# A 35,000-instruction transformer kernel: the second attention woven with the query projection, the rope angles moved forward, the last norm one tile ahead

## The reference

```python
cos, sin = rope_tables(positions)
...
proj = h @ w_q                                    # 1024 columns: 12 heads of 64, 256 memory query columns
q = apply_partial_rope(proj[..., :768], cos, sin) # rotates 16 of the 64 columns of a head
mix_out = sliding_window_attention(q, shared_k, shared_v, sinks)
mem_o = memory_attention(proj[..., 768:], mem_k, mem_v)
x = x + concatenate([mix_out, mem_o]) @ w_out
x = x + swiglu(rms_norm(x, ln_ffn), w_gate_up, w_down)
```

## Time and profile before

| | us |
|---|---|
| median of 3 runs | 2669.25 |
| lowest and highest | 2666.16, 2669.93 |
| the profiled execution, time | 2663.3 |
| the profiled execution, span | 2661.5 |
| TensorE busy | 2560.2 (96%) |
| VectorE busy | 1520.8 (57%) |
| ScalarE busy | 1043.8 (39%) |
| POOL busy | 978.9 (37%) |
| mean granted TensorE clock | 0.982 |

### The profile page before, as it was taken

The page is one execution under the profiler, slowest core; times in us unless marked ns, Lnnn a source line. Parts: engine busy times, 40 slices in busy tenths (PEclk is TensorE's granted clock), DMA queues, the critical chain, the costliest instruction groups (busy, mean ns, idle before and its releaser), DMA issues.

```text
span 2661.5 us, 35966 instructions
## 1 busy us (share of the span) xinstructions
PE 2560.2 (96%) x14072; PEld 2017.0 (76%) x14072; DVE 1520.8 (57%) x1968; ACT 1043.8 (39%) x1609; POOL 978.9 (37%) x259
## 2 busy tenths in 40 slices
PE   8999979999999899999989999999999998899998
PEld 7777938888877578888867777786658877688886
DVE  5736756542438746433266689973565784644244
ACT  5444544222232643222243355533454553432222
POOL 0346823444443024444433433341005552144443
PEclk9999979999999999999999999999999999899999
DMA  5225512222222012222233333334333332222222
GB/s 184 95 80 178 190 63 80 95 96 100 102 98 88 31 48 95 95 95 95 97 108 115 122 128 122 119 135 142 99 117 136 126 127 70 73 95 95 97 99 89
DMA packets 72391, 280.58 MB, mean 105 GB/s; under 512 B 9892, under 2 KB 27646, under 8 KB 45124
## 3 DMA queue, kind: packets, MB, share of 16 engines
q1 hardware_dynamic: 59875, 259.72, 28.7%
q10 hardware_dynamic: 12384, 19.03, 2.0%
HBM read 259.25 MB, written 19.40 MB: 105 GB/s over the span
## 4 chain that ended last, share of the span: by engine, by line
PE 71%; issue 17%; POOL 5%; DVE 4%; ACT 2%; DMA 0%; POOLq 0%; DVEq 0%; ACTq 0%; SPq 0%
PE banks L585 14%; PE banks L586 14%; PE banks L587 14%; POOL w_lo L3376 4%; PE banks L2752 2%; PE banks L1058 2%; PE banks L1057 2%; PE banks L1056 2%; PE banks L2760 2%; PE banks L1962 1%; PE banks L2863 1%; PE banks L2861 1%; PE banks L2862 1%; PE banks L2774 1%; PE banks L2507 1%
## 5 line engine op out<-in xcount | busy, mean ns | idle before, releaser
L3376 POOL TENSOR_TENSOR w_lo<-raw,w_hi 128x2048 fp32r<-128x2048 f32 x164 | 757.3, 4618 | 1337.9 <-ACT w_hi L564 1251.8
L585 PE MATMUL banks<-hn_hi,w_hi 128*128 128x512 f32 x1880 | 740.0, 394 | 21.0 <-DVE hn_lo L2275 7.8
L586 PE MATMUL banks<-hn_lo,w_hi 128*128 128x512 f32 x1880 | 735.5, 391 | 0.0
L587 PE MATMUL banks<-hn_hi,w_lo 128*128 128x512 f32 x1880 | 734.8, 391 | 0.0
L564 ACT ACTIVATE w_hi<-raw 128x2048 fp32r<-128x2048 f32 x180 | 345.0, 1917 | 607.4 <-PE banks L587 480.3
L585 PEld LDWEIGHTS banks<-hn_hi,w_hi 128*128 128x128 f32 x1880 | 355.1, 189 | 116.4 <-issue 32.5
L587 PEld LDWEIGHTS banks<-hn_hi,w_lo 128*128 128x128 f32 x1880 | 355.2, 189 | 74.7
L586 PEld LDWEIGHTS banks<-hn_lo,w_hi 128*128 128x128 f32 x1880 | 355.3, 189 | 72.6
L1001 DVE TENSOR_TENSOR hid_lo<-prod,hid_hi 128x512 f32 x62 | 281.4, 4538 | 117.8 <-ACT hid_hi L965 117.8
L998 DVE TENSOR_TENSOR prod<-sg,banks 128x512 f32<-128x512 f32 x62 | 42.6, 687 | 239.6 <-PE banks L587 239.6
L585 PE MATMUL banks<-hid_hi,w_hi 128*128 128x512 f32 x416 | 163.1, 392 | 3.3 <-POOL w_lo L3376 2.3
(11 more groups left out here) (582 smaller groups left out, 4064.8 us busy)
## 6 DMA issues: line engine op xcount, KB each, us to landing
raw<-in_W SPq DMA_DIRECT2D x202, 1024.0 KB, 4.8
oh_early<-codes SPq DMA_DIRECT2D x88, 128.0 KB, 3.0
extra<-in_W SPq DMA_DIRECT2D x8, 1024.0 KB, 4.7
spill<-cs ACTq DMA_DIRECT2D x32, 256.0 KB, 2.3
spill<-mem_q ACTq DMA_DIRECT2D x32, 256.0 KB, 2.7
oh_late<-codes SPq DMA_DIRECT2D x40, 128.0 KB, 2.8
grp<-spill SPq DMA_DIRECT2D x8, 512.0 KB, 4.5
grp<-spill SPq DMA_DIRECT2D x16, 256.0 KB, 4.8
```

The source lines that it names most:

```text
L585: pe.matmul(out, wh, xh(k), start=(k == 0), stop=False)
L586: pe.matmul(out, wh, xl(k), start=False, stop=False)
L587: mm = pe.matmul(out, wl, xh(k), start=False, stop=(k == nkt - 1))
L3376: pool.tensor_tensor(w_lo[:, u % 2, :], raw[:, u % 2, :], w_hi[:, u % 2, :].bitcast(F32), ALU.subtract).then_inc(S("w_lo"), 1)
```

## The change

1. **Weaving.** Query units 1 to 3 are done in half-jobs of 12 matmuls (half the k-steps of one output tile). After half-job q of unit i comes pair step 4i + q - 5, so that pairs 0 to 10 stand between the half-jobs, and pairs 11 to 18 (the last three without scores) follow as before. In a woven step TensorE makes values, transposes, scores, in this order. All woven scores use banks 2 and 3 (before, pairs took 4, 5 and 2, 3 in turn). The ropes stand where table `ROPES` says. ScalarE instead of VectorE evacuates the query tiles.
2. **Rope angles.** The 16 angle steps go behind the first six tiles of the down projection `dn02`: 3, 3, 3, 3, 2, 2. ScalarE issues the four loads ahead of that stage. The sines come directly behind the norm, before the next `prep_hi`.
3. **Last norm.** VectorE shifts tile j + 1 before it subtracts tile j.

```diff
+WOVEN = 11
+ROPES = {(0, 3): (6,), (1, 0): (0, 1), (1, 2): (2,), (2, 0): (3,), (2, 2): (4,), (3, 0): (5,)}
+ROPE_BANK = {6: 4, 0: 5, 1: 1, 2: 0, 3: 1, 4: 0, 5: 1}
+def pair_after(i, q):
+    p = 4 * i + q - 5
+    return p if 0 <= p < WOVEN else None
...
+    def pair_step(p):
+        if p < PAIRS:
+            for s in range(2):
+                k.add(("pair", p, s), (2 if p < WOVEN or p % 2 == 0 else 0) + s)
...
@@ dve_squares
+                if name == "dn02":
+                    rope_angles(v, min(16, 3 * k - max(0, k - 4)), min(16, 3 * k + 3 - max(0, k - 3)))
@@ act_ffn, down
+                    if f == 0:
+                        full(a, ("unit", U["dn01", 3], 1))
+                        for ap, load in ((rcol, "rcol"), (posi, "posi"), (perm, "perm"), (band, "band")):
+                            a.dma_start(ap[:, :], I[load]).then_inc(S("land_rope"), 16)
                     act_squares(a, name, ("norm", 3 + 3 * f), x_of, sq_tmp)
@@ dve_h2
+            shifted(0)
+            for j in range(KT):
+                if j + 1 < KT:
+                    shifted(j + 1)
+                taken(v, ("h2", j))
                 v.wait_ge(S("ada_hi"), KT + j + 1)
                 v.tensor_tensor(hn_lo[:, j, :], ring[:, j % 3, :], hn_hi[:, j, :].bitcast(F32), ALU.subtract)\
                     .then_inc(S("ada_lo"), 1)
...
+        def pe_pair_step(pe, p):
+            if WOVEN <= p < PAIRS:
+                pe_pair_scores(pe, p)
+            if p >= 3:
+                pe_pair_values(pe, p - 3)
+            if 2 <= p < PAIRS + 2:
+                pe_pair_turned(pe, p - 2)
+            if p < WOVEN:
+                pe_pair_scores(pe, p)
+        def pe_query_half(pe, i, q):
+            u, t = U["swaq", i], q // 2
+            key = ("unit", u, t)
+            if q == 0:
+                pe.wait_ge(S("w_lo"), u + 1)
+            hi, lo = W3(w_hi, u % 2), W3(w_lo, u % 2)
+            if q % 2 == 0:
+                open_bank(pe, key)
+            for k in range(4 * (q % 2), 4 * (q % 2) + 4):
...
+        def pe_queries(pe):
+            unit_jobs(pe, U["swaq", 0], 0, lambda k: t_hi[:, k, :], lambda k: t_lo[:, k, :], KT, ready=hn_ready(pe, 4))
+            pe_rope(pe, 6)
+            for i in range(1, 4):
+                for q in range(4):
+                    pe_query_half(pe, i, q)
+                    for j in ROPES.get((i, q), ()):
+                        pe_rope(pe, j)
+                    if pair_after(i, q) is not None:
+                        pe_pair_step(pe, pair_after(i, q))
+            for p in range(WOVEN, PAIRS + 3):
+                pe_pair_step(pe, p)
...
+        def act_pair_step(a, p):
+            if p < WOVEN and p >= 2:
+                act_pair_turned(a, p - 2)
+            if p < PAIRS:
+                act_pair_exps(a, p)
+            if p >= 3 and p % 2 == 0:
+                act_value(a, 1, (p - 4) // 2)
+            if WOVEN <= p < PAIRS + 2:
+                act_pair_turned(a, p - 2)
+        def act_queries_woven(a):
+            for t in range(2):
+                act_query(a, 0, t)
+            prep_hi(a, U["swaq", 0])
+            for i in range(1, 4):
+                for q in range(4):
+                    if q % 2:
+                        act_query(a, i, q // 2)
+                    if q == 3:
+                        prep_hi(a, U["swaq", i])
+                    if pair_after(i, q) is not None:
+                        act_pair_step(a, pair_after(i, q))
+            for p in range(WOVEN, PAIRS + 3):
+                act_pair_step(a, p)
...
@@ block.scalar
-            taken(a, ("unit", U["dn02", 3], 1))
-            for ap, name in ((rcol, "rcol"), (perm, "perm"), (band, "band"), (posi, "posi")):
-                a.dma_start(ap[:, :], I[name]).then_inc(S("land_rope"), 16)
             act_norm_round(a, 4)
+            rope_tables_act(a)
             prep_hi(a, U["kv", 0])
-            prep_hi(a, U["swaq", 0])
-            rope_tables_act(a)
-            for i in range(1, 4):
-                prep_hi(a, U["swaq", i])
-            act_pairs(a)
+            act_queries_woven(a)
```

More of the change, by code:

```diff
@@ L1355, in pe_attention, with pe_pair_scores @@
                         pe_modulation_turned(pe)
-        def pe_pairs(pe):
+        def pe_pair_scores(pe, p):
             items = attention_items(1)
[L1359 to L1366, removed]
-                    for s_ in range(2):
[L1368 to L1417, removed]
@@ new lines, in pe_pair_values @@
+        def pe_pair_values(pe, m):
+            items = attention_items(1)
+            for item in (2 * m, 2 * m + 1):
+                kind, t, b = items[item]
+                key = ("value", 1, item // NC)
+                if b == 0:
+                    open_bank(pe, key)
+                taken(pe, ("turn", 1, item))
+                first = 1 if kind == "swa" and not b else 0
+                for s_ in range(2):
+                    for m_ in range(first, 2):
+                        vh = mem_v[:, 1, m_, t * P:(t + 1) * P] if kind == "mem" else vs[:, b - 1 + m_, :]
+                        mm = pe.matmul(bank(key)[64 * s_:64 * s_ + 64, b * P:(b + 1) * P],
+                                       vh[:, 64 * s_:64 * s_ + 64],
+                                       pt[:, item % 2, (2 * s_ + m_) * P:(2 * s_ + m_ + 1) * P],
+                                       start=(m_ == first), stop=(m_ == 1), skip_group_check=True)
+                if b == NC - 1:
+                    mm.then_inc(fills(key), 1)
@@ new lines, in pe_pair_turned @@
+        def pe_pair_turned(pe, m):
+            items = attention_items(1)
+            for j in range(2):
+                item = 2 * m + j
+                kind, t, b = items[item]
+                key = ("turn", 1, item)
+                open_bank(pe, key)
+                pe.wait_ge(S("prob_normed"), 2 * ATT0 + 4 * m + 2 * j + 2)
+                for s_ in range(2):
+                    for half in range(1 if kind == "swa" and not b else 0, 2):
+                        c = 2 * s_ + half
+                        mm = pe.transpose(bank(key)[:, c * P:(c + 1) * P],
+                                          pr[:, m % 3, s_, j, half * P:(half + 1) * P], ident[:, :])
+                mm.then_inc(fills(key), 1)
@@ new lines, in dve_queries @@
+        def dve_queries(v):
+            taken(v, ("unit", U["kv", 0], 0))
+            dve_rope(v, 6)
+            for i in range(1, 4):
+                for q in range(4):
+                    for j in ROPES.get((i, q), ()):
+                        taken(v, ("unit", U["swaq", j // 2], j % 2))
+                        dve_rope(v, j)
+                    if pair_after(i, q) is not None:
+                        dve_pair_step(v, pair_after(i, q))
+            for p in range(WOVEN, PAIRS + 3):
+                dve_pair_step(v, p)
@@ new lines, in act_pair_turned @@
+        def act_pair_turned(a, m):
+            items = attention_items(1)
+            for item in (2 * m, 2 * m + 1):
+                kind, t, b = items[item]
+                key = ("turn", 1, item)
+                full(a, key)
+                turned = bank(key)[:, :].rearrange("p (s c) -> p s c", s=2)
+                probs = pt[:, item % 2, :].rearrange("p (s c) -> p s c", s=2)
+                first = P if kind == "swa" and not b else 0
+                a.activation(probs[:, :, first:256], turned[:, :, first:256], ACT.Copy).then_inc(reads(key), 1)
```

251 lines of the change are left out of this document (135 added, 116 removed).

## The result

The changed kernel takes 2675.62 us (median of 20 runs, 2670.31 to 2679.98) against 2668.34 us of the kernel before beside it (20 runs, 2660.56 to 2674.64): ratio 1.0026, 95% interval 1.0017 to 1.0035, so 7 us slower (4.5 to 9.3). The prediction said 2673.0 us in a range of 2663 to 2681, likeliest within 0.2%; the difference lies a little above that bound. The profiled executions took 2671.2 and 2663.3 us.

What follows compares the result with a forecast made beforehand. TensorE, 96% busy, was taken as the bound, with a POOL, VectorE and ScalarE ring limiting the down projection. +6.2 - 1.2 - 1.3 = +3.7 us on 2663.3 gave 2667.0, or 2673.0 on the timed runs' footing; range 2663 to 2681.

Steps and rivals of the forecast that it cites:

- slower by over 0.2%: Outcome for the whole kernel: slower by more than 5.3 us, chance 0.32.
- The ring: Down projection: POOL, VectorE and ScalarE wait for each other in turn, period 9.5 us, and set the pace.
- A: Distance: POOL's last low part start to key projection's first matmul. Rival: weave pays in full, about 2666, chance 0.22.
- Part 1: Rope angles moved into the down projection: costs about 6.2 us, bounds 3.5 to 8.
- caught: Down projection: third angle step behind tile 1 meets POOL's low part and waits until it ends; 2.2 us more.
- Part 2: Queries and attention woven: gives about 1.2 us, bounds +5.9 to -1.5 of gain.
- B: Distance: key projection's first matmul to output projection's. Rival: more angle steps run into POOL's time, 2675 or 2678, chance 0.26.
- block at pair 10: Woven attention: POOL's last low part holds VectorE's small step after pair 10's maximum for 3 us.
- C: Distance: output projection's first matmul to POOL's next low part. Rival: moved angles hidden, -2.5 us, 2667, chance 0.10.
- Part 3: Last norm one tile ahead: next unit starts earlier, gives 1.3 us, bounds 0.5 to 1.6.
- Sum: Whole kernel: +6.2 - 1.2 - 1.3 = +3.7 us against the kernel before.
- D: Distance in the last norm from its first matmul to the next unit's.

Runs made afterwards that it cites:

- late low part: The changed kernel with ScalarE's rounding of the second output-projection unit, and so POOL's low part, moved behind the last pair: 1.0012 of the kernel before.
- gaps, late, copies first: Changed kernel, ten angle steps in VectorE's waits, six behind keys and values, second output unit's low part behind last pair, pair 11's copies before exponentials: 0.9989, again 0.9983.
- the kernel with the angles back: The changed kernel with all 16 angle steps put back behind the key and value evacuation, weave and last norm kept: 1.0021 of the kernel before, again 1.0022.
- the run with the angles alone: The kernel before with only the position loads, sines and 16 angle steps moved as in the change: 1.0033 of the kernel before.

## Why the prediction was right, and where it was off

The time lies in the range, and the signs and sizes of the three parts hold. But "within 0.2%", with 0.50 the likeliest outcome, did not come: the result is in the branch "slower by over 0.2%" (0.32), and 2675.62 is just over the forecast's own range, 2670 to 2675 (whose lower end doesn't follow from +2 us, which gives 2671.3). The three terms account for less than half of the measured difference, so that the median lies in the range is owed in part to the range's width.

- **Bound.** The ring was the limit of the down projection: A grew by 6.0 us, by 6.3 alone, and by 0.1 when ten of the steps stood in its gaps and six behind the keys.
- **Part 1, +6.2.** Measured +6.0. The third step behind tile 1 was caught (5.78 us for two steps), and one step less there saved 2.25 us against the 2.2 said. The 3.7 us left without a catch lie at the lower bound of 3.5; the prediction also named 4.7 for that case, which is a us too much. The sum of the waits, "8 to 9", came as 7.2: behind the 5.26 us TensorE's unit ran at half clock (its first matmul 0.77 us), so it was itself later for the keys and waited less for them. The rule of the Trainium skill that the prediction weighed ("SBUF — State Buffer", "Who interferes with whom") gave the right one of the two sums, 6.2 and not 4.7: the trace agrees, with 5.78 us for two steps beside POOL and 2.86 for a small one.
- **Part 2, -1.2.** B is 1.5 us shorter (1.25 in the second trace). Its pieces: waits 1.68 and 0.95 (1.8 and 0.7 said), small step 2.86 (3), waits 2.80 and 4.05 (2.6 and 4.0), half clock behind them (said). What holds the second wait the prediction didn't say. The block at pair 10 does not: with the block gone it stayed 4.05 (late low part). Pair 10's maximum came 5.0 us earlier after the keys' start (5.9 said), pair 11's 2.3 (3.2 said). TensorE was 92% busy from 851 to 925, not over 95, since that stretch holds the 2.8 us wait too; without it, it is 96%. What I missed is C: in five of the nine traces of woven kernels, and in none of the three others, the output projection starts at half clock and loses 1.6 us.
- **Part 3, -1.3.** Measured 1.4, and a wait of 0.23 at the next unit. The rest of the 3.8 us in the trace is the clock.
- **Sum, +3.7.** The terms measure 6.0 - 1.5 - 1.4 = +3.1, and +4.7 with C (+3.3 in the second trace). The time says +7.0 and +8.0. A part of the rest stands in the traces, outside the four distances. Both traces of the changed kernel lose 2.8 to 2.9 us between 1335 and 1488 us, in the last block, where the code is unchanged. Half of it goes at one place: behind the same wait of 1.38 us the clock fell in the changed kernel and not before. Most of the rest goes behind a wait of 3.97 us that both have, where the half clock lasts 6.8 us instead of 3.4. Here is the first place in the changed kernel, then before (TensorE busy, matmuls, clock):

```profile
1408.00:1412.00 4.00, 4.00 (x11) 0.57 0.26 39
```
```profile
1400.00:1404.00 4.00, 4.00 (x18) 1.00 0.33 74
```

  With these the sums are +7.5 and +6.2, inside the intervals of the time. But one of the ten other traces has this loss too (gaps, late, copies first, the second timing), and the first timing of the same kernel has not. So whether the changed kernel meets it more often than before isn't shown.

  For the kernel with the angles back the traces have no such place: sums of +1.9 and +2.0, times of +5.6 and +5.9. Its profiled executions took 2666.4 and 2665.6 us, where its medians are 2673.2 and 2675.0, and they had more clock than the rest: 0.984 and 0.983, where the mean over its executions is 0.982 and 0.981. The slower halves of its executions take 7.4 and 6.7 us more than the faster ones, at a mean clock of 0.981 and 0.980 against 0.983 and 0.982. A mean lower by 0.002 of some 2670 us is about 10.7 us more at half clock, which is up to 5.3 us of time (an estimate from these numbers). So half clock is large enough for most of the missing 4 us. The changed kernel's executions have 0.981 in the mean, those of before beside its second timing 0.983. Where these spells lie, and why an order of work has more of them, no run shows.

Of the rivals, A (the weave pays in full) fell to the block at pair 10 and the pace behind it, C (angles hidden) to the run with the angles alone. B had the right sign and the wrong reason: no second catch came.

## What to carry to other kernels

Before work is put "beside" a stretch in which an engine idles, find whose wait ends last there. An engine can idle a quarter of the time and be on the ring; then a step's place decides, not its length (16 steps cost 6.0 or 3.7 us in the same stretch, and ten of them in its gaps 0.1). Price edits that serve each other together, and compare two traces by distances inside each: the unchanged code ahead of the edit moved by up to 14 us from one execution to another.

## What the runs showed of the hardware that I had not expected

- TensorE's granted clock can differ from one execution to the next at the same place of the same kernel. In the last norm the same kernel (gaps, late, copies first) had it at 0.50 behind its first matmul in one execution and not in the other, and D was 16.49 and 14.13 us:

```profile
2284.60 0.77 PE L603 MATMUL banks<-hn_hi,w_hi 128*128 128x512 f32 x1 [0.82 <-DVE hn_lo L1250]
2301.09 0.47 PE L603 MATMUL banks<-hn_hi,w_hi 128*128 128x512 f32 x1 [0.24 <-DVE w_lo L734]
```

- Most of an execution's lateness arises in the first layer's recurrence (230 to 320 us, some 2,000 small matmuls that wait for little but their issue). The changed kernel's second execution entered it 0.5 us ahead of the kernel before and left it 13 us behind. From 290 to 310 us its granted clock was 0.82 where before's was 1.00. Here that execution, then the kernel before (TensorE busy, matmuls, clock):

```profile
290.00:310.00 20.00, 16.05 (x372) 0.82 0.71 259
```
```profile
290.00:310.00 20.00, 18.18 (x336) 1.00 0.73 260
```
